# An SSD mixer with its decay counted from mid-sequence: far half as C times B for two heads at once, triangles added on TensorE

## What is computed

```python
def step(state, inp):
    xc, dtc, bc, cc = inp
    acum = jnp.cumsum(dtc * a, axis=1)
    diff = acum[:, :, None] - acum[:, None, :]
    decay = jnp.exp(jnp.where(causal, diff, -jnp.inf))
    cb = jnp.einsum('blgn,bsgn->blsg', cc, bc)
    scores = cb[..., None] * decay * dtc[:, None]
    y = jnp.einsum('blsge,bsgep->blgep', scores, xc)
    ...
y_fwd = ssd_scan(xs, dt[:, :, 0], a[0], b_in, c_in)
y_bwd = flip_seq(ssd_scan(flip_seq(xs), flip_seq(dt[:, :, 1]), a[1], flip_seq(b_in), flip_seq(c_in)))
y = y_fwd + y_bwd + xs * d_skip.astype(f32).reshape(SSD_GROUPS, SSD_HPG)[:, :, None]
```

## Time and profile before

| | us |
|---|---|
| median of 3 runs | 1387.13 |
| lowest, highest | 1386.33, 1388.41 |
| the profiled run | 1386.89 |
| its span, first to last instruction | 1385.1 |
| PE busy | 1356.7 (98%) |
| DVE, ACT, POOL busy | 820.9, 641.4, 639.2 |

### The profile page before, as it was taken

One profiled execution on the slowest core, in us unless ns is written; L12 is line 12 of the kernel. 1 busy time (PEld: TensorE's weight loads), 2 busy tenths in 40 slices (PEclk: granted clock), 3 DMA queues, 4 the chain that ended last, 5 costly groups with the idle time before them and its releaser, 6 DMA issues.

```text
span 1385.1 us, 16583 instructions
## 1 busy us (share of the span) xinstructions
PE 1356.7 (98%) x6642; PEld 1124.4 (81%) x6642; DVE 820.9 (59%) x977; ACT 641.4 (46%) x1017; POOL 639.2 (46%) x304
## 2 busy tenths in 40 slices
PE   7999999999999999999999999999999999999997
PEld 6778767878898888888889877887897888888886
DVE  5656596770067998886001755467279988883003
ACT  5553785543354544443223475544545444443221
POOL 2344693126524554455544244464625644554550
PEclk9999999999999999999999999999999999999999
DMA  6222100113313323323333323211322323323321
GB/s 208 92 83 89 38 1 23 47 64 104 92 46 135 94 92 97 101 89 96 87 97 89 118 61 92 90 34 46 106 92 92 91 96 103 92 89 96 97 84 62
DMA packets 36765, 117.89 MB, mean 85 GB/s; under 512 B 3856, under 2 KB 8336, under 8 KB 36688
## 3 DMA queue, kind: packets, MB, share of 16 engines
q1 hardware_dynamic: 35744, 114.38, 26.5%
q10 hardware_dynamic: 944, 2.45, 0.6%
...
## 4 chain that ended last, share of the span: by engine, by line
PE 89%; DVE 4%; ACT 3%; POOL 2%; issue 1%; DMA 0%; ACTq 0%; DVEq 0%
PE bank L327 26%; PE bank L329 26%; PE bank L328 26%; PE bank L1350 1%; PE bank L1353 1%; PE bank L1174 1%; PE bank L1879 1%; PE bank L1378 1%; PE bank L1897 1%; POOL ebuf L1010 1%; POOL wlo L310 1%; ACT ebuf L1098 1%; POOL ebuf L1006 1%; DVE xres L583 0%; PE bank L1598 0%
## 5 line engine op out<-in xcount | busy, mean ns | idle before, releaser
L310 POOL TENSOR_TENSOR wlo<-raw,whi 128x1024 fp32r<-128x1024 f32 (+2 forms) x215 | 528.7, 2472 | 666.0 <-ACT whi L304 665.8
L327 PE MATMUL bank<-xw_hi,whi 128*128 128x512 f32 (+1 forms) x1344 | 512.3, 381 | 12.6 <-DVE xw_lo L602 8.1
L329 PE MATMUL bank<-xw_hi,wlo 128*128 128x512 f32 (+1 forms) x1344 | 501.9, 373 | 0.0
L328 PE MATMUL bank<-xw_lo,whi 128*128 128x512 f32 (+1 forms) x1344 | 501.4, 373 | 0.0
L304 ACT ACTIVATE whi<-raw 128x1024 fp32r<-128x1024 f32 (+2 forms) x217 | 221.0, 1023 | 208.0 <-DMA raw<-in_fout 112.6
L327 PEld LDWEIGHTS bank<-xw_hi,whi 128*128 128x128 f32 x1344 | 254.9, 190 | 62.5 <-issue 16.4
L328 PEld LDWEIGHTS bank<-xw_lo,whi 128*128 128x128 f32 x1344 | 254.9, 190 | 47.6 <-issue 3.5
L329 PEld LDWEIGHTS bank<-xw_hi,wlo 128*128 128x128 f32 x1344 | 254.6, 189 | 45.6
L555 DVE RECIPROCAL small<-small 128x2 f32<-128x2 f32 (+1 forms) x12 | 2.0, 169 | 330.0 <-ACT small L487 319.5
L660 DVE SCALAR_TENSOR_TENSOR cbuf<-ubuf,par,cbuf 128x510 f32<-128x510 f32 x100 | 170.7, 1707 | 3.5
L327 PE MATMUL bank<-g_hi,whi 128*128 128x512 f32 (+1 forms) x396 | 146.2, 369 | 0.1
...
## 6 DMA issues: line engine op xcount, KB each, us to landing
...
xres<-in_x SPq DMA_DIRECT2D x8, 256.0 KB, 5.9
```

The costliest lines, as they stand in the source:

```text
L310: engine.tensor_tensor(wlo[s][:, 0:n], raw[s][:, 0:n], whi[s][:, 0:n].bitcast(F32), ALU.subtract).then_inc(w_lo, 1)
L327: first = nc.tensor.matmul(out_ap, wh, ah, start=start, stop=False)
L328: nc.tensor.matmul(out_ap, wh, al, start=False, stop=False)
L329: return first, nc.tensor.matmul(out_ap, wl, ah, start=False, stop=stop)
```

## The change

1. The running sum is counted from mid-sequence: `dve_dt` subtracts the value at token 127 (forward) or 128 (backward), two more steps on DVE between the sums and their fp32r parts.
2. Of the three tiles of a direction only the two on the diagonal are still made per head. The third, the far one, is the outer product of an l part (g = exp(A[l])) and an s part (w = exp(u[s])) times C.B. ACT makes g and w once for all heads (`act_dt_far`, four exponentials on 32 partitions, issued ahead of the first convolution). x by token is multiplied by w (`wx`: DVE in `dve_x_turn`, POOL in `pool_far` beside heads 3 to 6), PE multiplies it by plain C.B for two heads at once (`far_part` of `pe_ssd`, four fp32 matmuls of 128 columns), DVE multiplies the bank by `reach`, and `skip` adds it.
3. `reach` holds g of two heads, each on 64 partitions. SP writes g to DRAM (`gt_rows`), waits, and reads it back with each row repeated: four DMAs per two heads, issued between load(27) and load(28) (`REACH_AT` is 28). Those of pair c wait until pair c - 2 has been used.
4. The triangles are no factors any more: `pe_spread` first writes 0 or -2^30 into each bank (a fp32r matmul of `never_r` and four identities), and adds A to it, so the exponential gives 0 on the wrong side. The minima are gone; `cbm` is a plain copy of the bank.
5. ACT does seven exponentials per head: four of 128 columns forward, two of 128 backward and, for the later two blocks, one of 256 after DVE has added u to them (`dve_shift`).
6. Both directions are summed before C.B: `dve_both_ways` adds the backward bank to the forward tile (512 columns). POOL makes one product of 512 columns per head, DVE none, and `y` is four fp32 matmuls of 128 columns. `pe_spread` of head n + 2 now waits for `dve_both_ways` of head n.
7. DVE's old step L1064 becomes `skip` (same kind) and `near_part` (an addition); `far_part` on DVE is new. PE's sum of squares of the first group moves behind y of head 15. `cst` is 512 columns narrower.

```diff
...
+NEVER = -2.0 ** 30
...
+    ebuf = [sb(f"ebuf{i}", T, F32, s) for i in range(4)]
+    cbm = sb("cbm", 4 * T, F32, s)
...
+    reach = [sb(f"reach{i}", T, F32, s) for i in range(2)]
+    gt = sb("gt", T, F32, s, 64)
...
+    act_dt_far(act)
     turns(act, CONV0, SIDE, conv)
     act_mla_deviation(act)
...
+    act.wait_ge(sem("dt_dve"), 11)
...
         if j == 21:
-            dve_least(dve, 0)
...
-            dve_mask(dve, 0)
+            dve_shift(dve, 0)
+            dve_shift(dve, 1)
+            dve_both_ways(dve, 0)
         if j == 22:
...
+            dve_both_ways(dve, 1)
+            dve_shift(dve, 2)
...
+def far(t, d, past):
+    rows, at = slice(32 * d, 32 * d + 32), P if past != d else 0
+    return t[rows, :].rearrange("p (r s) -> p r s", r=NREQ)[:, :, at:at + P]
+gt_rows = nc.dram_tensor("gt_rows", (64, T), F32).ap()
+REACH_AT = next(f for f in range(TOTAL) if AFTER[f] >= BASE["mla"])
+def sp_reach(sp, c):
+    if c == 0:
+        sp.wait_ge(sem("dt_act"), 9)
+        sp.dma_start(gt_rows, gt[:]).then_inc(sem("gt_out"), 16)
+        sp.wait_ge(sem("gt_out"), 16)
+    if c >= 2:
+        sp.wait_ge(sem("ssd_far"), c - 1)
+    for u in range(2):
+        for d in range(2):
+            row, at = 32 * d + 2 * c + u, P * (1 - d)
+            to = req(reach[c % 2][u * HDIM:(u + 1) * HDIM, :])[:, :, at:at + P]
+            sp.dma_start(to, req(gt_rows[row:row + 1, :])[:, :, at:at + P].broadcast_to([HDIM, NREQ, P])).then_inc(
+                sem(f"reach_in{c % 2}"), 16)
+def act_dt_far(act):
+    act.wait_ge(sem("gt_zero"), 2)
+    act.wait_ge(sem("dt_dve"), 12)
+    for d in range(2):
+        nc.scalar.activation(far(w_f, d, 0), far(u_f, d, 0), ACT.Exp).then_inc(sem("dt_act"), 1)
+        nc.scalar.activation(far(gt, d, 1), far(a_f, d, 1), ACT.Exp).then_inc(sem("dt_act"), 1)
...
+        rows, at = slice(32 * d, 32 * d + 32), P - 1 + d
+        total = req(sum_f[rows, :])
+        step(nc.vector.tensor_tensor(req(a_f[rows, :]), total,
+                                     total[:, :, at:at + 1].broadcast_to([32, NREQ, SEQ]), ALU.subtract))
...
     dve.wait_ge(sem("cb_mm"), i + 1)
...
+    nc.vector.tensor_copy(cbm[:, i * T:(i + 1) * T], bank[6][:]).then_inc(sem("cb_set"), 1)
+    dve.wait_ge(sem("xtok_act"), i + 1)
+    dve.wait_ge(sem("dt_dve"), 13)
+    nc.vector.tensor_tensor(by_head(wx[0], i), by_head(bank[4], 0), far_weight(i, 0), ALU.mult).then_inc(
+        sem("wx_dve"), 1)
...
+    e = ebuf[n % 4][:].rearrange("p (r x) -> p r x", r=NREQ)
+    own = cbm[:, (n // 8) * 2 * T:(n // 8 + 1) * 2 * T].rearrange("p (r q x) -> p r q x", r=NREQ, q=4)
+    pool.wait_ge(sem("ssd_both"), n + 1)
+    nc.gpsimd.tensor_tensor(e.rearrange("p r (s x) -> p r s x", s=2), e.rearrange("p r (s x) -> p r s x", s=2),
+                            own[:, :, 0::3], ALU.mult).then_inc(sem("ssd_m"), 1)
+def pool_far(pool, i):
+    pool.wait_ge(sem("cb_set"), NBLK)
+    pool.wait_ge(sem("xtok_dve"), i + 1)
+    pool.wait_ge(sem("dt_dve"), 13)
+    nc.gpsimd.tensor_tensor(by_head(wx[1], i), by_head(xtok[1], i), far_weight(i, 1), ALU.mult).then_inc(
+        sem("wx_pool"), 1)
...
+def dve_shift(dve, n):
     dve.wait_ge(sem("a_mm"), 2 * n + 2)
...
+    if n == 0:
+        dve.wait_ge(sem("dt_dve"), 13)
+    later = abank(n, 1)[:, SEQ:2 * SEQ].rearrange("p (s x) -> p s x", s=2)
+    u_s = cols[:].rearrange("p (b w n) -> p b w n", b=NBLK, w=2)[:, 2:4, 1, 32 + n]
+    nc.vector.tensor_tensor(later, later, u_s.unsqueeze(2).broadcast_to([P, 2, P]), ALU.add).then_inc(
+        sem("ssd_shift"), 1)
+def dve_both_ways(dve, n):
+    dve.wait_ge(sem("ssd_exp"), EXPS * (n + 1))
+    nc.vector.tensor_tensor(ebuf[n % 4][:], ebuf[n % 4][:], abank(n, 1)[:], ALU.add).then_inc(
+        sem("ssd_both"), 1)
 def dve_ssd(dve):
+    def far_part(c):
+        dve.wait_ge(sem("far_mm"), c + 1)
+        dve.wait_ge(sem(f"reach_in{c % 2}"), 64 * (c // 2 + 1))
+        nc.vector.tensor_tensor(bank[6][:], bank[6][:], reach[c % 2][:], ALU.mult).then_inc(sem("ssd_far"), 1)
+    def skip(c):
+        dve.wait_ge(sem("ssd_far"), c + 1)
+        nc.vector.scalar_tensor_tensor(out=ck(xbc, c), in0=ck(xbc, c), scalar=prm("dskip", c),
+                                       in1=bank[6][:], op0=ALU.mult, op1=ALU.add).then_inc(
+                                           sem("ssd_skip"), 1)
+    def near_part(c):
+        dve.wait_ge(sem("y_mm"), 2 * c + 2)
+        dve.wait_ge(sem("ssd_skip"), c + 1)
+        nc.vector.tensor_tensor(ck(xbc, c), ck(xbc, c), bank[4 + c % 2][:], ALU.add).then_inc(sem("ssd_y"), 1)
...
+        c = n // 2
+        if n % 2:
+            far_part(c)
+        elif n:
+            near_part(c - 1)
+        if n + 2 < HEADS:
+            dve_both_ways(dve, n + 2)
         if n + 3 < HEADS:
...
+            dve_shift(dve, n + 3)
+        if n % 2:
+            skip(c)
+        elif n:
+            gated(c - 1)
     dve_mla_low(dve)
     dve_mla_rotated(dve)
+    near_part(KD - 1)
...
+    act.wait_ge(sem("a_mm"), 2 * n + 1)
     if n == 0:
...
+        act.wait_ge(sem("dt_dve"), 13)
     if n >= 4:
         act.wait_ge(sem("y_mm"), n - 3)
...
+    for b in range(NBLK):
+        at = slice(b * P, (b + 1) * P)
+        nc.scalar.activation(ebuf[n % 4][:, at], abank(n, 0)[:, at], ACT.Exp, bias=u_s(b, 0)).then_inc(
+            sem("ssd_exp"), 1)
+    act.wait_ge(sem("ssd_shift"), n + 1)
+    for b in range(2):
+        o = abank(n, 1)[:, b * P:(b + 1) * P]
+        nc.scalar.activation(o, o, ACT.Exp, bias=u_s(b, 1)).then_inc(sem("ssd_exp"), 1)
+    o = abank(n, 1)[:, SEQ:2 * SEQ]
+    nc.scalar.activation(o, o, ACT.Exp).then_inc(sem("ssd_exp"), 1)
...
-        pe.wait_ge(sem("ssd_exp"), 8 * n - 8)
+        pe.wait_ge(sem("ssd_both"), n - 1)
     for d in range(2):
         pick = ident_r[:, 32 * d + n:32 * d + n + 1].to_broadcast([P, P])
...
+        nc.tensor.matmul(abank(v, d)[:].rearrange("p (b x) -> p b x", b=NBLK), never_r[:, d * P:(d + 1) * P],
+                         eye_r[:].unsqueeze(1).broadcast_to([P, NBLK, P]), start=True, stop=False)
+        nc.tensor.matmul(abank(v, d)[:], pick, at_both[:], start=False, stop=True).then_inc(sem("a_mm"), 1)
...
+        if c == 0:
+            pe.wait_ge(sem("wx_dve"), NBLK)
+            pe.wait_ge(sem("hin_u"), 23)
+        else:
+            pe.wait_ge(sem("ssd_skip"), c)
+        if c == 4:
+            pe.wait_ge(sem("wx_pool"), NBLK)
+        for r in range(NREQ):
+            for s in range(2):
+                b, cb_at = 2 * r + s, (2 * (c // 4) + r) * T + (1 + s) * P
+                w_at, o_at = b * T + (c % 4) * P, r * SEQ + (1 - s) * P
+                last = nc.tensor.matmul(bank[6][:, o_at:o_at + P], wx[c // 4][:, w_at:w_at + P],
+                                        cbm[:, cb_at:cb_at + P], start=True, stop=True)
+        last.then_inc(sem("far_mm"), 1)
     def y(n):
         c, u = n // 2, n % 2
...
         pe.wait_ge(sem("ssd_m"), n + 1)
...
         if c >= 2 and u == 0:
             pe.wait_ge(sem("ssd_y"), 2 * c - 3)
...
+        for b in range(NBLK):
+            at, x_at = slice(b * P, (b + 1) * P), b * T + (c % 4) * P + u * HDIM
+            last = nc.tensor.matmul(bank[4 + c % 2][u * HDIM:(u + 1) * HDIM, at],
+                                    xtok[c // 4][:, x_at:x_at + HDIM], ebuf[n % 4][:, at], start=True,
+                                    stop=True)
         last.then_inc(sem("y_mm"), 1)
     for n in range(HEADS):
         if n + 3 < HEADS:
             pe_spread(pe, n + 3)
+        if n % 2 == 0:
+            far_part(n // 2)
         if n == HEADS - 1:
             pe_mla_prep(pe)
         y(n)
-        if n == 14:
...
+    pe.wait_ge(sem("ssd_skip"), KD)
+    pe.wait_ge(sem("ssd_acc"), 3)
+    nc.tensor.matmul(bank[6][:], ones[:, 0:P], group_rstd[0][:], start=True, stop=True).then_inc(
+        sem("ssd_ss"), 1)
...
+        if f == REACH_AT:
+            for c in range(KD):
+                sp_reach(sp, c)
```

More of the change, by code:

```diff
@@ L849, in dve_hin @@
             dve.wait_ge(sem("ident_in"), 16)
+            dve_picks(dve)
             for j in range(2 * Z0, 24):
@@ L887, in build_program @@
         group_rstd = [rstd, sqacc]
-        dt_f, dta_f, a_f = (ebuf[0][0:64, i * T:(i + 1) * T] for i in range(3))
-        u_f = dta_f
+        dt_f, dta_f, sum_f, a_f = (wx[0][0:64, i * T:(i + 1) * T] for i in range(4))
+        u_f, w_f = (sqbuf[i][0:64, :] for i in range(2))
         DT_LEAST = 1e-30
@@ L932, in dve_dt @@
             done(7)
+            for d in range(2):
+                rows, at = slice(32 * d, 32 * d + 32), P - 1 + d
+                total = req(sum_f[rows, :])
+                step(nc.vector.tensor_tensor(req(a_f[rows, :]), total,
+                                             total[:, :, at:at + 1].broadcast_to([32, NREQ, SEQ]), ALU.subtract))
+            done(9)
             step(nc.vector.tensor_copy(at_both[0:64, :], a_f))
-            done(8)
+            done(10)
```

(43 more changed lines are left out.)

105 lines of the change are left out of this document (28 added, 77 removed).

## The result

| | before | after |
|---|---|---|
| median | 1386.57 (6 runs) | 1392.07 (6 runs, 1391.56 to 1393.30) |
| the profiled run | 1386.89 | 1391.95 |
| its span | 1385.1 | 1390.1 |
| block 23 of the projection ends | 159.70 | 168.12 |
| first product of MLA | 215.92 | 219.35 |

A forecast was written before the change was run, and what follows sets the result against it. PE was taken as the bound, with DVE and POOL close behind. Stage -9.9, triangles +1.4 and dt steps +2.2 gave -6.3 us: 1380.8 us from 1386.89 profiled (median of runs 0.24 higher), range 1376 to 1390 for 8 in 10.

The forecast's parts named there:

- Triangles ahead of the stage: Spreads 0, 1 and 2 between PE's projection blocks: two triangle matmuls each, 6 x 0.23 = 1.4 us lost.
- The dt steps: Ahead of first convolution: two subtractions 1.3, four exponentials 1.5, less 0.6: 2.2 us lost; table load free, otherwise 1.3 more.
- The copies in `dve_picks`: Ahead of the stage: lie in idle DVE time, each under 1.5 us beside blocks of 5.4; no cost unless cover fails.
- The way to `reach`: From block 23's end: load, g to DRAM and back, 2.7 + 2.3 + 2.3 = 7.3 us; PE waits 3.7 before head 5's spread.
- Its clock: Behind PE's 3.7 us wait in the stage: half clock may follow, 1.0 us taken off the saving.
- The beat: SSD heads: all four engines need 2.4 to 2.5 us per head, PE 2.43; 2.5 taken, where PE needed 3.41.
- that rival: DVE not relieved: `dve_both_ways` takes 1.35 to 1.65 us against POOL; 8 to 12 us more, say 1391; chance 0.10.
- The end of the stage: Last pairs of heads: DVE needs about 6.5 to 8 us where PE needs about 6; PE waits 1.5.
- Behind the stage: MLA and what follows: PE work as before, moving as a whole; no change in length.
- reach late: Before the first far part: reach lands at 12 instead of 7.3 us, 4.7 more, 1385.5; chance 0.10.
- the ring: Heads sharing banks: spread, exponentials, sum, next spread wait on each other, 3.1 us per head; 7 more, 1388; chance 0.12.
- the clock: Whole stage: PE stops a little every head and gets 1.2 GHz, 4.9 us per head; 28 more, 1409; chance 0.04.

The follow-up runs named there:

- all four edits: Changed kernel with copies behind third turn, far exponentials behind first convolutions, first two reach ahead of load(22), gate read from PSUM bank: 1375.14 us, ratio 0.9913.

## Why the prediction was wrong

The sum was -9.9 + 1.4 + 2.2 = -6.3; the trace has -5.0 for the stage, +8.4 ahead of it, and 1.6 more in the span behind MLA's start. The 11.3 between them are 4.2 for the copies, 1.0 for the dt steps, 4.9 in the stage and 1.6 behind it, less 0.4.

- *Triangles ahead of the stage*: 1.4 forecast, 1.4 measured.
- *The dt steps*: 2.2 forecast, 3.2 measured. The subtractions (1.39) and the exponentials (1.5) were right. Of the two answers offered for the table load, free or 1.3, the free one was taken, and the other came; with it the sum would be 3.5, near the 3.6 of added work.
- *The copies in `dve_picks`*: nothing forecast, 4.2 measured. **This is the step that failed.** It moved two copies from a place where POOL stood still and a row of before had their price, 0.40, to one beside three POOL products. "Each under 1.5 us beside blocks of 5.4" went by the size of the operations. The cover was real when they began and gone before they ended, because they ended when POOL did. The price of lost cover was named ("they would cost as much once"), but for 1.5 us and not for 4.75. The Trainium skill, "SBUF — State Buffer", section "SBUF: two separate sides", says that a DVE operation in a two-port mode, and not only one with two SBUF inputs, takes a lock exclusive of GpSimd's, and names copies and casts among those that can run in such a mode. The trace agrees with a lock, 4.75 beside POOL against 0.40 alone; that these casts ran in that mode no row shows. The prediction had used that section for `dve_both_ways` and the gate, and not asked it about the copies.
- *The way to `reach`*: 7.3 forecast, 7.8 measured (168.12 to 175.91). The third wait, its place and its size (3.7 forecast, 3.99) came as written. Its clock did not: spread, far part and y behind it took 5.50 us (177.25 to 182.75) and take 3.10 in the kernel with all four edits (167.96 to 171.06), so 2.4 instead of 1.0. The 1.0 was read from one window of before, 54 to 56 us; the next, 56 to 58, has 0.68, so that gap of 2.46 had cost 1.6 already.
- *The beat*: 2.5 per head forecast, 2.74 measured on DVE. The gate's 0.96 was right for the kernel before, where seven of eight gates last 0.98 to 1.00 because each met the last 0.45 us of a POOL product; it was taken as the gate's own price. In the new order it meets the whole product, 1.64. Everything else on DVE was as forecast (sum 0.68, far 0.69, skip 0.74, near 0.69, shift 0.43), so `dve_both_ways` did not contend, and that rival failed as it was put; its mechanism held in the gate. Of the two rows held against that rival one was misread: L1532 never ran beside a POOL product in the kernel before, so its 0.69 said nothing about contention. Once the gate reads a bank, PE is the bound at 2.59. Most of the rest over 2.43 is y: 1.02 us for eight records, priced at 0.87 from transposes; `far_part` takes 0.98 for two heads, where 0.87 was put down.
- *The end of the stage*: a wait of 1.5 forecast, 2.47 measured (most of it DVE's slower beat, which PE pays here and not head by head), and from there to MLA 7.23 us at a falling clock against 5.60 with all four edits (198.32 to 203.92). That 1.6 had no term.
- *Behind the stage*: "MLA and what follows move as a whole" was not quite so. PE waits 0.98 us for `diag` in both kernels (at 952.15 before, at 955.18 after), and only after has a granted clock of 0.87 from 950 to 960, where before has 1.00. The next 24 projection matmuls take 7.2 us (956.95 to 964.15) instead of 5.6 (953.93 to 959.55): 1.6.

Of the rivals, *reach late* and *the ring* did not happen, *the clock* fell in five short stretches, behind each of the four waits and at 957 us, and not through the stage. The right mechanisms were nearly all on the page; what failed was to give one of them no price and to take the cheap end for two others.
